# The V half of the expert loop loaded in 1 MB units of four expert blocks into two slots, in place of 512 KB units of two blocks into four slots

## What is computed

```python
def peer_ffn(h, lp):      # h: 512 tokens x 2048; 16384 experts, 128 chosen per token
    ...                   # product keys choose eidx and gates, 8 heads x 16
    def one_block(args):
        xb, eb, gb = args
        act = jnp.einsum('td,ted->te', xb, u_tab[eb])
        act = jax.nn.gelu(act, approximate=False) * gb
        return jnp.einsum('te,ted->td', act, v_tab[eb])
```

## Time and profile before

| | us |
|---|---|
| median of 3 timed runs | 3674.06 |
| fastest and slowest of them | 3669.34, 3677.08 |
| profiled execution, span | 3671.1 |
| PE busy | 3492.4 (95%) |
| DVE busy | 2836.4 (77%) |
| ACT busy | 1178.4 (32%) |
| POOL busy | 1152.9 (31%) |

### The profile page before, as it was taken

How to read it: one execution, slowest core, us unless ns; L and a number is a source line. 1 busy time by engine, 2 the same in 40 slices (tenths; PEclk the granted TensorE clock), 3 DMA queues, 4 the chain that set the end, 5 groups by cost and what they waited for, 6 DMA issues and landing times.

```text
span 3671.1 us, 58994 instructions
## 1 busy us (share of the span) xinstructions
PE 3492.4 (95%) x20872; PEld 3090.0 (84%) x20872; DVE 2836.4 (77%) x3738; ACT 1178.4 (32%) x1917; POOL 1152.9 (31%) x1002
## 2 busy tenths in 40 slices
PE   7999999999996999997899999999999999999996
PEld 3688888888885876467899999999999999999995
DVE  2566665666566225989799999999999999999997
ACT  1222322322332221119433333333333333333331
POOL 1444444444442523211222222222222222222231
PEclk9999999999998999999999999999999999999998
DMA  9444434434434423225999999999999999999995
GB/s 384 168 139 142 131 116 146 137 126 140 137 126 168 176 80 126 103 80 173 344 376 368 379 367 379 368 375 373 365 379 367 379 370 365 381 367 378 368 371 222
DMA packets 233659, 957.82 MB, mean 261 GB/s; under 512 B 23050, under 2 KB 64618, under 8 KB 158210
## 3 DMA queue, kind: packets, MB, share of 16 engines
q1 hardware_dynamic: 171730, 541.78, 39.9%
q0 software_dynamic: 55296, 402.68, 28.6%
q10 hardware_dynamic: 6576, 12.65, 1.1%
HBM read 918.06 MB, written 33.65 MB: 259 GB/s over the span
## 4 chain that ended last, share of the span: by engine, by line
DVEq 21%; DVE 18%; issue 6%; ACT 5%; PE 3%; ACTq 0%
DVEq L2179 20%; DVE Ub L2177 6%; DVE acc_r L2188 3%; ACT UH L1304 3%; DVE UL L1309 2%; DVE acc_x L2188 2%; DVE VL L1329 1%; DVE acc_d L2172 1%; DVE GB L2134 1%; ACT AHa L2072 1%; PE PS L2005 1%; PE PS L2006 1%; PE PS L2007 1%; ACT coef L2078 0%; ACT coef L2080 0%
## 5 line engine op out<-in xcount | busy, mean ns | idle before, releaser
L2006 PE MATMUL PS<-AL,VH 128*128 128x320 f32 x2048 | 637.6, 311 | 0.0
L1337 PE MATMUL PS<-xl,UH 128*128 128x320 f32 x2016 | 622.9, 309 | 0.0
L1338 PE MATMUL PS<-xh,UL 128*128 128x320 f32 x2016 | 622.9, 309 | 0.0
L1336 PE MATMUL PS<-xh,UH 128*128 128x320 f32 x2016 | 622.4, 309 | 0.0
L398 PE MATMUL PS<-hH,WH 128*128 128x512 f32 (+1 forms) x1312 | 479.0, 365 | 1.1 <-ACT mvT L667 1.0
L399 PE MATMUL PS<-hL,WH 128*128 128x512 f32 (+1 forms) x1312 | 461.1, 351 | 0.0
L400 PE MATMUL PS<-hH,WL 128*128 128x512 f32 (+1 forms) x1312 | 460.8, 351 | 0.0
L1958 POOL DMA_INDIRECT Vb<-peer_v,stage x192 | 212.0, 1104 | 753.0 <-DVE acc_r L2188 504.8
L1958 POOL DMA_INDIRECT Ub<-peer_u,stage x192 | 227.8, 1187 | 598.7 <-DVE Ub L2177 561.5
L2006 PEld LDWEIGHTS PS<-AL,VH 128*128 128x128 f32 x2048 | 387.8, 189 | 0.2 <-issue 0.2
L2005 PE MATMUL PS<-AHa,VH 128*128 128x320 f32 x1024 | 325.1, 317 | 64.0 <-DVE acc_d L2172 27.5
(11 more groups left out here) (344 smaller groups left out, 7174.4 us busy)
## 6 DMA issues: line engine op xcount, KB each, us to landing
VR<-peer_vt SPq DMA_DIRECT2D x256, 512.0 KB
UR<-peer_ut SPq DMA_DIRECT2D x126, 1024.0 KB
AW<-wada SPq DMA_DIRECT2D x128, 512.0 KB, 3.8
WR<-wseq SPq DMA_DIRECT2D x224, 256.0 KB, 2.6
wr<-wmod SPq DMA_DIRECT2D x32, 1024.0 KB, 10.2
gates_dram<-GS SPq DMA_DIRECT2D x10, 2048.0 KB, 8.9
GB<-gates_dram SPq DMA_DIRECT2D x31, 640.0 KB
oR<-wout SPq DMA_DIRECT2D x32, 512.0 KB, 3.3
```

The source lines that it names most:

```text
L1336: pe.matmul(dst, high[:, j % 2, k, :], xh[:, k, :], start=(k == 0), stop=False)
L1337: pe.matmul(dst, high[:, j % 2, k, :], xl[:, k, :], start=False, stop=False)
L1338: last = pe.matmul(dst, low[:, j % 2, k, :], xh[:, k, :], start=False, stop=(k == KT - 1))
L2006: pe.matmul(low, VH[:, slot, j, cols], AL[:, :, b, :], start=False, stop=False)
```

## The change

V's unit becomes four blocks by 512 columns, 1 MB, so that a partition's piece is 8 KB. A turn has four units `c` = 0 to 3, one for each quarter, and two slots. The array `peer_vt` is laid out for it on the host. ACT and DVE still split half a unit at a time (`v_half`), in the order of before. TensorE reads the same data in the same order. SP waits for the whole quarter (`s_po`) alone; the semaphore `s_va` and its increments go. In a turn SP issues four V transfers instead of eight, each where the second of a pair was.

```diff
-SLOTS = 4
+VSLOTS = 2
-        VR = over("VR", "ring_place", [P, SLOTS, GROUP, CHUNK], skip=8 * GROUP * D)
+        VR = over("VR", "ring_place", [P, VSLOTS, SUPER, CHUNK], skip=8 * GROUP * D)
-        def v_unit(sp, m, u):
-            unit = peer_vt[bass.ds(8 * m + 4 * (u % 2) + u // 2, 1), :, :]
-            sp.dma_start(VR[:, u % 4, :, :].rearrange("p b d -> p (b d)"), unit.rearrange("a p f -> p (a f)")).then_inc(s_vb[u % 4], 16)
+        def v_unit(sp, m, c):
+            unit = peer_vt[bass.ds(OUT_CHUNKS * m + c, 1), :, :]
+            sp.dma_start(VR[:, c % VSLOTS, :, :].rearrange("p b d -> p (b d)"), unit.rearrange("a p f -> p (a f)")).then_inc(s_vb[c % VSLOTS], 16)
+        def v_half(u):
+            return slice(GROUP * (u % 2), GROUP * (u % 2) + GROUP)
         def v_high(act, s, u):
-            act.wait_ge(s_vb[u % 4], 16 * (2 * s + u // 4) + 16)
-            act.activation(VH[:, u % 4, :, :], VR[:, u % 4, :, :], ACT.Copy).then_inc(s_vh, 1)
+            c = u // 2 % VSLOTS
+            act.wait_ge(s_vb[c], 16 * (2 * s + u // 4) + 16)
+            act.activation(VH[:, c, v_half(u), :], VR[:, c, v_half(u), :], ACT.Copy).then_inc(s_vh, 1)
...
-                        sp.wait_ge(s_va, 4 * s + 1); v_unit(sp, s, 4)
-                        sp.wait_ge(s_po, KT * s + 4); v_unit(sp, s, 5)
+                        sp.wait_ge(s_po, KT * s + 4); v_unit(sp, s, 2)
                         extra(0)
                         if more:
                             sp.wait_ge(s_pa, SUPER * s + SUPER + 1); u_block(sp, s + 1, 2)
                             gates(s + 1)
-                        sp.wait_ge(s_va, 4 * s + 2); v_unit(sp, s, 6)
-                        sp.wait_ge(s_po, KT * s + 8); v_unit(sp, s, 7)
+                        sp.wait_ge(s_po, KT * s + 8); v_unit(sp, s, 3)
...
-                        slot = (2 * r + h) % 4
+                        slot = r % VSLOTS
...
-                        if h == 0:
-                            last.then_inc(s_va, 1)
```

More of the change, by code:

```diff
@@ L1256, in program @@
         s_gst = [sem("gate_chunk_stored0"), sem("gate_chunk_stored1")]
-        s_vb = [sem(f"v_chunk_loaded{c}") for c in range(OUT_CHUNKS)]
+        s_vb = [sem(f"v_unit_loaded{c}") for c in range(VSLOTS)]
         s_g0 = sem("first_gates_kept")
@@ L1309, in u_low @@
             eng.tensor_tensor(low[:, j % 2, :, :], raw[:, j % 2, :, :], high[:, j % 2, :, :].bitcast(f32), ALU.subtract).then_inc(s_ul, 1)
-        VR = over("VR", "ring_place", [P, SLOTS, GROUP, CHUNK], skip=8 * GROUP * D)
+        VR = over("VR", "ring_place", [P, VSLOTS, SUPER, CHUNK], skip=8 * GROUP * D)
         chunk = [slice(c * CHUNK, (c + 1) * CHUNK) for c in range(OUT_CHUNKS)]
-        def v_unit(sp, m, u):
-            unit = peer_vt[bass.ds(8 * m + 4 * (u % 2) + u // 2, 1), :, :]
-            sp.dma_start(VR[:, u % 4, :, :].rearrange("p b d -> p (b d)"), unit.rearrange("a p f -> p (a f)")).then_inc(s_vb[u % 4], 16)
-        VL = over("VL", "ring_place", [P, SLOTS, GROUP, CHUNK], f32r, skip=8 * GROUP * D)
-        VH = over("VH", "ring_place", [P, SLOTS, GROUP, CHUNK], f32r, skip=12 * GROUP * D)
+        def v_unit(sp, m, c):
+            unit = peer_vt[bass.ds(OUT_CHUNKS * m + c, 1), :, :]
+            sp.dma_start(VR[:, c % VSLOTS, :, :].rearrange("p b d -> p (b d)"), unit.rearrange("a p f -> p (a f)")).then_inc(s_vb[c % VSLOTS], 16)
+        VL = over("VL", "ring_place", [P, VSLOTS, SUPER, CHUNK], f32r, skip=8 * GROUP * D)
+        VH = over("VH", "ring_place", [P, VSLOTS, SUPER, CHUNK], f32r, skip=12 * GROUP * D)
+        def v_half(u):
+            return slice(GROUP * (u % 2), GROUP * (u % 2) + GROUP)
         s_vh, s_vl = sem("v_high_parts"), sem("v_low_parts")
         def v_high(act, s, u):
-            act.wait_ge(s_vb[u % 4], 16 * (2 * s + u // 4) + 16)
-            act.activation(VH[:, u % 4, :, :], VR[:, u % 4, :, :], ACT.Copy).then_inc(s_vh, 1)
+            c = u // 2 % VSLOTS
+            act.wait_ge(s_vb[c], 16 * (2 * s + u // 4) + 16)
+            act.activation(VH[:, c, v_half(u), :], VR[:, c, v_half(u), :], ACT.Copy).then_inc(s_vh, 1)
         def v_low(dve, s, u):
             dve.wait_ge(s_vh, 8 * s + u + 1)
-            dve.tensor_tensor(VL[:, u % 4, :, :], VR[:, u % 4, :, :], VH[:, u % 4, :, :].bitcast(f32), ALU.subtract).then_inc(s_vl, 1)
+            c = u // 2 % VSLOTS
+            dve.tensor_tensor(VL[:, c, v_half(u), :], VR[:, c, v_half(u), :], VH[:, c, v_half(u), :].bitcast(f32), ALU.subtract).then_inc(s_vl, 1)
         def dense_dots(pe, m, j):
@@ L1453, in _ @@
                     sp.wait_ge(s_pairs, 1)
-                    for u in range(4):
-                        v_unit(sp, 0, u)
+                    for c in range(VSLOTS):
+                        v_unit(sp, 0, c)
                     sp.wait_ge(s_ef, 1)
@@ L1877, in program @@
         s_gb, s_gm, s_gh = sem("gates_loaded"), sem("dots_gated"), sem("gated_high_parts")
-        s_va, s_po = sem("first_pairs_multiplied"), sem("dense_outputs")
+        s_po = sem("dense_outputs")
         s_m, s_add = sem("dense_gated"), sem("dense_added")
@@ L1915, in turn @@
                             sp.wait_ge(s_pa, SUPER * s + SUPER + 2); u_block(sp, s + 1, 3)
-                            sp.wait_ge(s_va, 4 * s + 3); v_unit(sp, s + 1, 0)
-                            sp.wait_ge(s_po, KT * s + 12); v_unit(sp, s + 1, 1)
+                            sp.wait_ge(s_po, KT * s + 12); v_unit(sp, s + 1, 0)
                             if more2:
                                 sp.wait_ge(s_pa, SUPER * s + SUPER + 3); u_block(sp, s + 2, 0)
-                            sp.wait_ge(s_va, 4 * s + 4); v_unit(sp, s + 1, 2)
-                            sp.wait_ge(s_po, KT * s + KT); v_unit(sp, s + 1, 3)
+                            sp.wait_ge(s_po, KT * s + KT); v_unit(sp, s + 1, 1)
                             if more2:
@@ L2004, in out_part @@
                             b = GROUP * h + j
-                            pe.matmul(dst, VH[:, slot, j, cols], AH[b][:] if h else AHa[:, j, :], start=(b == 0), stop=False)
-                            pe.matmul(low, VH[:, slot, j, cols], AL[:, :, b, :], start=False, stop=False)
-                            last = pe.matmul(dst, VL[:, slot, j, cols], AH[b][:] if h else AHa[:, j, :], start=False, stop=(b == SUPER - 1))
+                            pe.matmul(dst, VH[:, slot, b, cols], AH[b][:] if h else AHa[:, j, :], start=(b == 0), stop=False)
+                            pe.matmul(low, VH[:, slot, b, cols], AL[:, :, b, :], start=False, stop=False)
+                            last = pe.matmul(dst, VL[:, slot, b, cols], AH[b][:] if h else AHa[:, j, :], start=False, stop=(b == SUPER - 1))
                             if b == SUPER - 1:
                                 last.then_inc(s_po, 1)
-                        if h == 0:
-                            last.then_inc(s_va, 1)
                     def turn(s, more):
@@ L2342 @@
         "peer_ut": con(np.asarray(peer_u)[0].reshape(NEB, P, KT, P).transpose(0, 3, 2, 1)),
-        "peer_vt": con(np.asarray(peer_v)[0].reshape(NEB // GROUP, GROUP, P, OUT_CHUNKS, CHUNK).transpose(0, 3, 2, 1, 4).reshape(NEB // GROUP * OUT_CHUNKS, P, GROUP * CHUNK)),
+        "peer_vt": con(np.asarray(peer_v)[0].reshape(NS, SUPER, P, OUT_CHUNKS, CHUNK).transpose(0, 3, 2, 1, 4).reshape(NS * OUT_CHUNKS, P, SUPER * CHUNK)),
         "consts": consts, "rope": rope,
```

## The result

The changed kernel takes 3694.24 us (median of 5 runs, 3689.01 to 3700.77) against 3677.08 us for the kernel before (5 runs). The ratio is 1.0049, 95% interval 1.0034 to 1.0063: it is slower by 17 us, where no change was forecast. The profiled execution's span is 3692.5 us, 21.4 us more than before.

The account below looks back on a forecast made before the run. DVE's chain, with round trips to ACT, was taken to set the turn. All terms were 0, so the span stayed 3671.1 us, plus 3 us to the timed median: 3674; own range 3668 to 3681, 8 in 10 from 3665 to 3691.

Parts of the forecast that it names:

- What bounds the kernel: Loop turn of 58.11 us: DVE's chain, with its round trips to ACT, sets it; DMA engines and PE do not.
- That V's transfers could only lose time: V's loads in the loop: coming earlier gives nothing, coming after DVE's turn for them costs all of the delay.
- Unit 3: Merged 6 and 7, behind the gates' load: lands within 9.85 us of issue, just in time; cost 0, upper end 3 us.
- The share of the queues: V beside GpSimd's gathers: a third of 415 GB/s with 4 KB pieces, a half with 8 KB, so 1.049 MB takes 5.05 us.
- Unit 0: Merged 0 and 1: even landing no sooner than old unit 1, DVE's part is ready at 2683.6, needed 2685.26; cost 0.
- The slower rival: Merged unit 3 lands when old unit 7 did, some 1.5 us late in ten turns: 3689, or up to 3699; chance 0.22.
- The gathers: GpSimd's queue beside V: they pay for V's larger share, 0.8 us, and get it back; cost 0, some 3 us cover.
- the other units: Old units 2 and 3, and 4 and 5, landed before ACT came to them; cost 0.
- the last turn: No `dense_dots` between quarters: DVE begins 2.7 us later, taken up by its 3.88 us stand for PE; cost 0.
- The faster rival: Better V transfers shorten the turn: 3595 at most, or 3664 if U's or the gathers' transfers took part; chance 0.08.

Follow-up runs that it names:

- before_uearly: The kernel before with two steps exchanged on ACT: U blocks 1 and 3 are rounded ahead of weighing dots 0 and 3; 3631.61 us, ratio 0.9878.
- merged_reordered: The changed kernel with looser order at units 0 and 3: ACT weighs dots 2 and 4 earlier, DVE subtracts V's low parts later; 3677.42 us, ratio 1.0008.
- merged_4k: The changed kernel with V in DRAM as before, so one 1 MB transfer moves two 4 KB pieces per partition; 3740.37 us, ratio 1.0173.
- early_whole: The kernel before with one more wait: ACT begins a quarter's first half only when the second half has landed too; 3691.34 us, ratio 1.0048.

## Why the prediction was wrong

**What bounds the kernel: right.** DVE's chain sets the turn; before_uearly took 45 us of DVE's waits for the rounding of U away (46.0 to 1.2 us) and got 44. That V's transfers could only lose time was right too: merged_reordered has no stand for V left in the window and is no faster than before.

**Unit 3: the time nearly right, by two errors that cancel.** Unit 3 cost 4.3 us, where 0 to 3 were given. One of its late landings, issue and ACT's start in the changed kernel:

```profile
2555.52 0.33 SPq L1317 DMA_DIRECT2D VR<-peer_vt  x1
...
2565.57 1.06 ACT L1329 ACTIVATE VH<-VR 128x1024 fp32r<-128x1024 f32 x1 [6.99 <-DMA VR<-peer_vt]
```

That is 10.0 us after the issue, and DVE stood 1.12 us, so in this turn it wanted the unit 8.9 us after the issue and not 9.85. What SP's queue moved, 2557.5 to 2558.5, 2558.5 to 2562 and 2562 to 2565.5:

```profile
q1 hardware_dynamic: 3, 0.01, 1.3%
...
q1 hardware_dynamic: 103, 0.82, 62.4%
...
q1 hardware_dynamic: 41, 0.23, 15.7%
```

The forecast had the queue busy with the gates until 4.8 us after the issue and the unit then landing in 5.05. The queue ran empty, the unit began 3.0 us after its issue, and it took 7.0. The sum came out near (10.0 for 9.85) by luck.

**The share of the queues: the direction right, the reading wrong.** The forecast took the 3.78 us between the landings of units 6 and 7 for the time in which 0.524 MB moved, at 139 GB/s, a third of 415. But from 1970.5 to 1973.5, between which unit 6 landed, the queues of the kernel before moved this:

```profile
q0 software_dynamic: 154, 1.15, 95.1%
q1 hardware_dynamic: 15, 0.05, 4.4%
```

From 1973.5 to 1975.5 SP's queue moved 0.50 MB in 65 packets, of which three at most were of 4 KB; the rest is a U block's. So nearly all of unit 7 had moved before 1970.5, and the 3.78 us are what its last pieces took. 139 GB/s is no rate of the queue, and a half of 415 was not seen either. That a larger piece helps is shown, by merged_4k: +65 us with pieces of 4 KB, +17 with 8. An estimate that fits: SP's queue took 0.041 us of one engine for each KB (39.2% of 16 engines for 269.89 MB), so a piece of 4 KB takes 0.17 us and one of 8 KB 0.34. If each engine has eight of a unit's 128 rows, and the last one takes a piece of V and one of the gathers in turn, 0.5 MB in 4 KB pieces needs 8 x 0.51 = 4.1 us there (3.78 between the landings), and 1 MB needs 8.2 in 4 KB pieces but 5.4 in 8 KB pieces. No run shows the engines one by one.

**Unit 0: the step that failed.** "Even if the merged unit landed no sooner than unit 1 did, DVE's part would be ready at 2683.6", costed at 0. The bound was no bound. Unit 1 landed 8.0 us after its issue because it had only its own 0.5 MB left to move; unit 0's had gone ahead of it, up to the 3 us in which unit 1's transfer was starting. A unit issued whole at unit 1's time starts then and moves both. It landed 11.0 us after the issue in the turn shown, and the stands at unit 0 make 15.2 of the 19.5 us. The forecast gave no argument for this bound. Its argument for unit 3 (the queue is busy with what stands ahead, so a later issue loses nothing) would not have held either: at unit 0 only a U block stands ahead, which lands 2.4 us after the issue in the turn shown, before the new transfer has begun.

**The slower rival: right in size, by another mechanism.** It gave 3689 by unit 3 landing with unit 7 in ten turns. That is what early_whole does (3691.34). In the changed kernel the larger pieces save unit 3 for the most part, and unit 0 is late instead.

**The gathers, the other units, the last turn: right.** No row of DVE's waits names a gather or units 1 and 2. The last turn did not get longer, though DVE stood 4.46 us for V there, 1.3 us more than before (2.7 were given). DVE's stand of 3.88 us for PE, which was to take this up, is gone whole, and the turn became 2.9 us shorter:

```profile
3634.85 1.23 DVE L1334 TENSOR_TENSOR VL<-VR,VH 128x1024 fp32r<-128x1024 f32 x1 [4.46 <-ACT VH L1329]
```

**The faster rival** did not come, for the reason given. ACT's waits for V grew from 79 to 265 us in 1800 to 3560 (over 100 was said). Most of that cost nothing: DVE stood 19.5 us.

## What to carry to other kernels

When two transfers become one at the time of the second, the first loses its head start: work out the landing anew, from the start of the transfer, for every place where it is issued, and don't take the second's old landing for a bound. Whether it costs is decided by the engine that leads and by the slack ahead of its use; two edits that cost 15 and 5 us by themselves cost 68 together. A landing seen before is the time of the last piece and not a rate: look at what the queue moved in between. Where transfers of two queues run beside each other, look at the size of the pieces of the one that is waited for: beside gathers of 8 KB rows, 8 KB in place of 4 KB took this loss from 65 to 17 us. Sizes beyond these two were not tried. And a wait of the leading engine that comes back every turn, here 0.75 us behind a step on another engine that had no need to stand there, was worth more than the whole question of the transfers.

## What the runs showed that was not expected

The landing of a 1 MB transfer beside gathers has a long tail. In the turn shown 0.75 MB of it moved in 2.5 us, the last 0.18 MB in 3.5 us; for the unit 3 shown it was 0.82 MB in 3.5 us and the last 0.23 MB in 3.5. A landing worked out from a mean over the 16 engines, as the forecast did (half of 415 GB/s, 5.05 us), comes some 2 us too early for both. Which engine is last, and why, these runs don't show.

A transfer that SP issues moves next to nothing until some 3 us later, in all three cases looked at: those issued at 2686.97 and 2555.52 in the changed kernel and at 2674.51 in the kernel before. It can't be for want of a free engine alone: in 2557.5 to 2558.5 the two queues filled 88% of the engines' time (86.8% the gathers, 1.3% SP's), and SP's moved 0.01 MB.
